# The scan of a Mamba-2 layer, written channel-major: two heads side by side, two gate projections moved into the convolution loop, fixed PSUM banks

## The reference, cut to what matters

```python
proj = h @ w_in                       # 1024 -> z 2048 | xbc 2560 | dt 32
z, xbc, dt = split(proj)
xbc = silu(causal_depthwise_conv(xbc, conv_w, conv_b))        # 4 taps
xs, bm, cm = split(xbc)               # x: 32 heads of 64; B, C: 2 groups of 128
dt = softplus(dt + dt_bias);  a = -exp(a_log)
# scan in two chunks of 128 tokens (c = 0, 1); l, s are tokens within a chunk
a_cs   = cumsum(dt * a)
decay  = exp(a_cs[l] - a_cs[s]) for s <= l, else 0
y_diag = einsum(C B^T, decay, x * dt)                         # within a chunk
states = einsum(B, exp(a_cs[last] - a_cs), x * dt)            # chunk 0's end state
y_off  = einsum(C, states, exp(a_cs))                         # into chunk 1
y = y_diag + y_off + d_skip * xs
g = y * silu(z);  g = g * rsqrt(mean(g*g per group) + eps) * norm_w
out = g @ w_out                       # 2048 -> 1024
```

## Time and profile before

| | us |
|---|---|
| median of 3 runs (lowest to highest) | 1395.65 (1393.22 to 1397.87) |
| the profiled execution, its own time | 1398.21 |
| its span | 1396.4 |
| TensorE busy | 1333.6 (95%) |
| VectorE busy | 855.3 (61%) |
| ScalarE busy | 666.5 (48%) |
| mean granted TensorE clock | 0.981 of full speed |

### The profile page before, as it was taken

The page is one execution under the profiler, slowest core; times in us unless marked ns, Lnnn a source line. Parts: engine busy times, 40 slices in busy tenths (PEclk is TensorE's granted clock), DMA queues, the critical chain, the costliest instruction groups (busy, mean ns, idle before and its releaser), DMA issues.

```text
span 1396.4 us, 20308 instructions
## 1 busy us (share of the span) xinstructions
PE 1333.6 (95%) x8604; PEld 1212.5 (87%) x8604; DVE 855.3 (61%) x1125; ACT 666.5 (48%) x834; POOL 40.5 (3%) x59
## 2 busy tenths in 40 slices
PE   5999999999999999998997999999999999999997
PEld 5888789999899889997997988899989888899996
DVE  4677665554554665555898786655555776665553
ACT  4454454443354454443765554544444545454442
POOL 2000000000000000000101110000000000000000
PEclk9899999999999999999998999999998999999999
DMA  7643365556554475552773444655525143375540
GB/s 239 169 126 141 101 216 191 187 194 192 157 155 143 166 239 187 194 169 91 240 231 108 137 160 139 231 195 192 186 87 211 54 143 130 123 246 190 181 151 31
DMA packets 147834, 231.06 MB, mean 165 GB/s; under 512 B 7651, under 2 KB 116493, under 8 KB 147744
## 3 DMA queue, kind: packets, MB, share of 16 engines
q1 hardware_dynamic: 144896, 221.66, 48.0%
q0 software_dynamic: 2848, 8.10, 2.7%
HBM read 227.08 MB, written 2.65 MB: 165 GB/s over the span
## 4 chain that ended last, share of the span: by engine, by line
PE 78%; DVE 13%; ACT 5%; issue 2%; DMA 2%; POOL 0%; SPq 0%; DVEq 0%; POOLq 0%; ACTq 0%
PE bank L501 13%; PE bank L503 13%; PE bank L502 13%; PE acc L697 11%; PE acc L698 10%; PE acc L701 10%; DVE wlo L484 5%; ACT whi L474 3%; PE bank L855 2%; DMA raw<-in_mla_w_in 1%; DMA raw<-in_mla_w_ukv 1%; PE bank L630 1%; PE bank L1305 1%; ACT junk L523 1%; DVE cacc L1503 1%
## 5 line engine op out<-in xcount | busy, mean ns | idle before, releaser
L484 DVE TENSOR_TENSOR wlo<-raw,whi 128x2048 fp32r<-128x2048 f32 (+1 forms) x209 | 466.8, 2245 | 195.6 <-ACT whi L474 195.5
L474 ACT ACTIVATE whi<-raw 128x2048 fp32r<-128x2048 f32 (+1 forms) x209 | 387.7, 1869 | 89.7 <-PE acc L701 79.3
L501 PE MATMUL bank<-hhi,whi 128*128 128x256 f32 x1448 | 414.5, 286 | 6.3 <-DVE xn L1575 3.7
L502 PE MATMUL bank<-hlo,whi 128*128 128x256 f32 x1448 | 411.3, 284 | 0.0
L503 PE MATMUL bank<-hhi,wlo 128*128 128x256 f32 x1448 | 411.2, 284 | 0.0
L501 PEld LDWEIGHTS bank<-hhi,whi 128*128 128x128 f32 x1448 | 278.3, 192 | 12.3 <-issue 8.2
L502 PEld LDWEIGHTS bank<-hlo,whi 128*128 128x128 f32 x1448 | 278.4, 192 | 3.3 <-issue 1.0
L503 PEld LDWEIGHTS bank<-hhi,wlo 128*128 128x128 f32 x1448 | 278.3, 192 | 0.2
L697 PE MATMUL acc<-whi,uhi 128*128 128x512 f32 x512 | 200.0, 391 | 1.8 <-DVE ulo L816 1.8
L698 PE MATMUL acc<-wlo,uhi 128*128 128x512 f32 x512 | 200.0, 391 | 0.0
L701 PE MATMUL acc<-whi,ulo 128*128 128x512 f32 x512 | 159.3, 390 | 0.0
(11 more groups left out here) (213 smaller groups left out, 1676.9 us busy)
## 6 DMA issues: line engine op xcount, KB each, us to landing
raw<-in_mlp_w SPq DMA_DIRECT2D x128, 1024.0 KB, 5.3
raw<-in_ssd_w_in SPq DMA_DIRECT2D x18, 1024.0 KB, 6.1
raw<-in_mla_w_o SPq DMA_DIRECT2D x16, 1024.0 KB, 5.6
raw<-in_mla_w_ukv SPq DMA_DIRECT2D x8, 1024.0 KB, 6.2
raw<-in_moba_w_qkv SPq DMA_DIRECT2D x16, 512.0 KB, 5.5
raw<-in_ssd_w_out SPq DMA_DIRECT2D x8, 1024.0 KB, 5.0
raw<-in_mla_w_uq SPq DMA_DIRECT2D x8, 768.0 KB, 8.7
raw<-in_mla_w_in SPq DMA_DIRECT2D x4, 1024.0 KB, 8.3
```

The lines of the kernel that those rows point to most:

```text
L474: nc.scalar.activation(whi[:, s, :e], raw[:, s, :e], ACT.Copy).then_inc(w_hi_done[s], 1)
L484: nc.vector.tensor_tensor(wlo[:, s, :e], raw[:, s, :e], whi[:, s, :e].bitcast(F32), ALU.subtract).then_inc(w_split[s], 1)
L501: nc.tensor.matmul(ps, lhs[0], rhs[0], start=start, stop=False)
L502: nc.tensor.matmul(ps, lhs[0], rhs[1], start=False, stop=False)
```

## The change: what it does

- Instead of [token, channel] the scan's outputs are formed as [channel, token]: the stationary operand is a head's `xdt` (128 tokens x 64 channels), the moving one its decays (128 x 128). Two heads write the lower and the upper 64 partitions of one bank ("side by side"). The transposes back ("yT"), the copies to `y_sb` and their sum fall away.
- The state is no longer formed. Chunk 0's part in chunk 1 is a product of `dxdt` with a third block `cross` = exp(running sum) times C1 B0^T (`cbx`), which is loaded by GpSimd, taken through exp by ScalarE and multiplied by `cbx` by VectorE in each round.
- The subtraction in the decays becomes a maximum over a whole 128 x 1024 block on VectorE, and the difference goes into ScalarE's exp as a bias, which needs one instruction per head: 16 of 128 x 128 a round.
- The gate projections z0 and z1 stand in the convolution loop after cv5 and cv7, as do the decays and inputs of round 0. Gates of round q are finished in round q+1; the output units 4 to 7 follow scan 3.
- Banks are fixed: y in 0 and 1, xT and z in 2 and 3; cv8 in 1, cv9 in 2.
- The sums of squares move from GpSimd to VectorE (`gate_sum`).
- Which unit is split where is written out by hand (`split_early`, `split_late`).

```diff
-        prevT = xn[:, 1, 512:1024]
-        y_sb = junk[:].rearrange("p (c n) -> p c n", c=T)
+        cross = junk[:].rearrange("p (h n) -> p h n", h=8)
...
+            def gate_unit(n, bank=None):
+                unit(("z", n), KD, 256, cols(w, 256 * n, 256 * (n + 1)))
+                jobs.add(("z", n), bank, ready=used(("z", n)))
+
+            def turned_inputs(q):
+                jobs.add(("xT", q, 0), 2)
+                jobs.add(("xT", q, 1), 3)
+
             for n in range(10):
...
-                jobs.add(("cv", n), ready=used(("cv", n)))
+                jobs.add(("cv", n), {8: 1, 9: 2}.get(n), ready=used(("cv", n)))
...
+                if n in (5, 7):
+                    gate_unit((n - 5) // 2)
+                if n == 7:
+                    turned_inputs(0)
+            for q in range(4):
                 if q:
+                    gate_unit(2 * q, 2)
+                    gate_unit(2 * q + 1, 3)
+                jobs.add(("y", 2 * q), 0)
+                jobs.add(("y", 2 * q + 1), 1)
+                if q < 3:
+                    turned_inputs(q + 1)
                 for n in out_units[q]:      # now {0: [], 1: [0, 1], 2: [2, 3], 3: [4, 5, 6, 7]}
                     unit(("so", L, n), 2, DM, rows(A["ssd_w_out"][0], 256 * n, 256 * (n + 1)))
...
+            split_early = {1: so[1], 2: ("z", 5), 3: ("z", 7)}
+            split_late = {1: ("z", 5), 2: so[3], 3: so[5]}
...
+            def scan(n):
+                q = n // 2
+                ps = open_job(te, ("y", n))
+                for i in range(2):
+                    hh = [4 * (n % 2) + 2 * i + a for a in range(2)]
+                    ch = [slice(h * SSD_HD, (h + 1) * SSD_HD) for h in hh]
+                    dst = [ps[a * SSD_HD:(a + 1) * SSD_HD, i * SEQ:(i + 1) * SEQ] for a in range(2)]
+                    for a in range(2):
+                        nc.tensor.matmul(dst[a][:, tok(0)], xdt[:, 0, ch[a]], dec[:, (2 * q) % 4, hh[a], :],
+                                         start=True, stop=True)
+                    for a in range(2):
+                        nc.tensor.matmul(dst[a][:, tok(1)], xdt[:, 1, ch[a]], dec[:, (2 * q + 1) % 4, hh[a], :],
+                                         start=True, stop=False)
+                    for a in range(2):
+                        mm = nc.tensor.matmul(dst[a][:, tok(1)], dxdt[:, ch[a]], cross[:, hh[a], :],
+                                              start=False, stop=True)
+                mm.then_inc(ready(("y", n)), 1)
...
+            for q in range(4):              # TensorE, after cv9
                 if q:
                     proj(("z", 2 * q))
                     proj(("z", 2 * q + 1))
+                job_copied(te, ("xT", q, 0))
+                job_copied(te, ("xT", q, 1))
+                te.wait_ge(dx_done, q + 1)
+                te.wait_ge(dec_ready, 2 * (q + 1))
+                te.wait_ge(cross_ready, q + 1)
+                scan(2 * q)
+                scan(2 * q + 1)
+                if q < 3:
+                    turn_inputs(q + 1)
                 for n in out_units[q]:
...
+                if q >= 2:
+                    sums(q - 2)
...
+            def decays(q):                  # ScalarE
+                for c in range(T):
+                    b = (2 * q + c) % 4
+                    act.wait_ge(dec_diff, 2 * q + c + 1)
+                    for hh in range(8):
+                        ins = nc.scalar.activation(dec[:, b, hh, :], dec[:, b, hh, :], ACT.Exp, scale=-1.0,
+                                                   bias=tokv[:, 2 + c, 8 * q + hh:8 * q + hh + 1])
+                    ins.then_inc(dec_exp, 1)
+
+            def cross_decay(q):
+                act.wait_ge(cross_loaded, 16 * (q + 1))
+                nc.scalar.activation(cross, cross, ACT.Exp, scale=-1.0).then_inc(cross_exp, 1)
...
+                if n in (5, 7):             # in ScalarE's convolution loop, behind silu(n - 1)
+                    gate_silu((n - 5) // 2)
+                if n == 5:
+                    decays(0)
+                    cross_decay(0)
...
+            decays(1)
+            for q in range(1, 5):
+                for n in (2 * q - 2, 2 * q - 1):
+                    gate_square(n)
+                    gate_hi(n)
                 if q < 4:
+                    cross_decay(q)
+                    if q < 3:
+                        decays(q + 1)
+                    act_splits(act, split_early[q], 0)
+                    gate_silu(2 * q)
+                    gate_silu(2 * q + 1)
+                    act_splits(act, split_late[q], 0)
+            act_splits(act, ("so", L, 7), AHEAD - 1)
...
+                if n in (4, 6):             # in VectorE's convolution loop, behind conv(n)
+                    diffs((n - 4) // 2)
+                if n in (5, 7):
+                    dve_splits(dve, ("z", (n - 5) // 2))
+                if n == 7:
+                    decay_cb(0, 0)
+                    decay_cb(0, 1)
+                    cross_cb(0)
+                if n == 8:
+                    scaled_inputs(0)
...
+            for q in range(1, 5):
                 if q < 4:
+                    scaled_inputs(q)
+                for n in (2 * q - 2, 2 * q - 1):
+                    gate(n)
+                if q == 1:
+                    decay_cb(1, 0)
+                    decay_cb(1, 1)
+                for n in (2 * q - 2, 2 * q - 1):
+                    gate_sum(n)
+                    gate_lo(n)
                 if q < 4:
                     if q < 3:
                         diffs(q + 1)
+                    cross_cb(q)
                     if q < 3:
                         decay_cb(q + 1, 0)
                         decay_cb(q + 1, 1)
+                    dve_splits(dve, split_early[q], 0)
+                    if q == 3:
+                        mean_square(0)
+                        half_residual()
+                    dve_splits(dve, split_late[q], 0)
+            dve_splits(dve, ("so", L, 7), 0)
+            mean_square(1)
+            dve_splits(dve, ("so", L, 7), AHEAD - 1)
```

More of the change, by code:

```diff
@@ L179, in build @@
         headc = sb("headc", [SSD_H, 4])
-        tokv = sb("tokv", [P, 6, SSD_H])
+        tokv = sb("tokv", [P, 5, SSD_H])
         g_ms = sb("g_ms", [P, SSD_G, T])
@@ L228, in build @@
             CT = sb("CT", [P, SSD_G, SEQ], F32, stage)
-            Btok = sb("Btok", [P, SSD_G, P], F32, stage)
+            cbx = sb("cbx", [P, SSD_G, P], F32, stage)
             cbm = sb("cbm", [P, SSD_G, T, P], F32, stage)
@@ L381, in plan_ssd @@
                     jobs.add("cb")
[L382 to L386, removed]
-                if q:
[L388 to L399, removed]
-                if q in (2, 4):
-                    jobs.add(("ss", q // 2 - 1))
+                    jobs.add("cbx")
+                if n in (5, 7):
[3 more added lines that the diff above has]
+            for q in range(4):
+                if q:
+                    gate_unit(2 * q, 2)
[4 more added lines that the diff above has]
+                    turned_inputs(q + 1)
                 for n in out_units[q]:
                     unit(("so", L, n), 2, DM, rows(A["ssd_w_out"][0], 256 * n, 256 * (n + 1)))
+                if q >= 2:
+                    jobs.add(("ss", q - 2), 3)
         bias_in_mla = "moba" in kinds and kinds[0] == "mla"
@@ L1260, in build @@
         DT, EXP, U, LN, DD, DEC, DTO, ACS = range(8)
+        so_of = {L: {n: ("so", L, n) for n in range(8)} for kind, L, i in stages if kind == "ssd"}
+        split_early, split_late = {}, {}
+        for so in so_of.values():
+            split_early = {1: so[1], 2: ("z", 5), 3: ("z", 7)}
+            split_late = {1: ("z", 5), 2: so[3], 3: so[5]}
         def pe_ssd(te, j, L):
@@ L1340, in pe_ssd @@
+                        mm = nc.tensor.matmul(ps[:, g * P:(g + 1) * P], BT[:, g, tok(0)], CT[:, g, tok(1)],
+                                              start=True, stop=True)
+                    mm.then_inc(ready("cbx"), 1)
+                if n in (5, 7):
+                    proj(("z", (n - 5) // 2))
+                if n == 7:
+                    turn_inputs(0)
+            for q in range(4):
+                if q:
                     proj(("z", 2 * q))
-                    te.wait_ge(dx_done, q + 1)
@@ new lines, in half_residual @@
+            def half_residual():
+                dve.wait_ge(grstd_done, 1)
+                for t in range(T):
+                    if t == 0:
+                        dve.wait_ge(acc_done, acc_rounds[j])
+                    else:
+                        dve.wait_ge(*used(("so", L, 3)))
+                    for half in range(2):
+                        c = slice(512 * half, 512 * half + 512)
+                        nc.vector.scalar_tensor_tensor(out=x[:, t, c], in0=acc[t][half][:],
+                                                       scalar=g_rstd[:, 0, t:t + 1], in1=x[:, t, c], op0=ALU.mult,
+                                                       op1=ALU.add).then_inc(ssd_half, 1)
```

288 lines of the change are left out of this document (99 added, 189 removed).

## The result

The changed kernel takes 1421.15 us (median of four runs, 1418.78 to 1421.76) beside 1396.72 us (four runs, 1393.22 to 1397.87): 1.0172 times as long, 95% interval 1.0157 to 1.0187. It is slower, as forecast, but by 24.4 us where 14.5 were forecast, and outside the range of 1399 to 1417. The profiled execution took 1421.76 us, its span is 1419.7 us and its mean clock 0.976; before they were 1398.21, 1396.4 and 0.981. So 23.3 us of span are to be found.

What follows compares the result with a forecast made beforehand. TensorE, 95% busy, was taken to bound the kernel. The terms -14.1 + 10.7 + 2.1 + 9.0 + 6.8 = +14.5 us, on the median 1395.65, gave a forecast of 1410 us, range 1399 to 1417.

Steps and rivals of the forecast that it cites:

- The three waits: TensorE idle in the SSD stage: 8.2 us before cv9, 6.5 us before z6, 4.1 us before so6.
- late at the residual: Behind so6, VectorE still has so7, up0 and up1 to split and reaches the residual 0.7 us late.
- Nothing outside this stage changes: Outside the SSD stage the kernel stays as it was; no time was entered for it.
- TensorE's own work: In the scan, a round falls from 6.1 to 5.2 us: 3.7 us less over four rounds, 0.2 added for `cbx`.
- the overlap: In the scan, the two heads of a pair overlap wholly, so a round takes 2.6 us; chance 0.28.
- The rival: Scan pairs overlap; of 4 x 2.6 us only 3.8 us come out, giving 1406 us; chance 0.28.
- The short waits: Round 1: TensorE waits 0.35 us before z2 and 1.8 us before scan 2 of the rounds, 2.1 us together.
- The small exps: ScalarE's decays: 16 exps of 128 columns at 0.25 us each, 4.1 us a round; upper end 6.4.
- the rival of 0.40 us: Small exps cost 0.40 us, each `decays` 2.4 us longer, +4.8 us in all, giving 1415 us; chance 0.12.
- The drain of 1.38 us: ScalarE's table reload: by the skill's estimate, the two chains with a reload would each be about 1.38 us longer.
- The clock: Low TensorE clock behind the waits: +2.5 us after cv9, +2.5 after z6, +2.0 after so6 (0 to 2.5).
- old losses: SSD stage of the old order: waits and low clock lose 3.1 + 3.7 + 2.9 + 0.9 = 10.6 us, all gained.

Runs made afterwards that it cites:

- split_early: Changed kernel with the weight splits of z7 and so7 moved so that they don't stand behind `gate_hi`: 1402.86 us, ratio 1.0047.
- xt_early: Changed kernel with `scaled_inputs(0)`, which frees bank 2, placed on VectorE ahead of the block products: 1412.58 us, ratio 1.0116.
- layout_before: Kernel before the change with its tiles moved 128 bytes lower, where the changed kernel has them: 1404.22 us, ratio 1.0056.
- same_half: Changed kernel with one head's three scan products, then the other's, all written to the lower 64 partitions: 1417.36 us in its one run.
- old_decays: Changed kernel with the earlier decays: small subtractions with a maximum on VectorE and two large exps a round on ScalarE: 1413.21 us, ratio 1.0120.
- pairs_apart: Changed kernel with the three scan products of one head issued first, then the three of the other: 1417.81 us, ratio 1.0153.
- layout_back: Changed kernel with `tokv` given its sixth row again, so later tiles lie where they lay before the change: 1410.92 us, ratio 1.0104.

## Why the prediction was right or wrong

**The three waits: right.** cv9 0.83 + 7.76 us (8.2 forecast), z6 6.71 (6.5), so6 4.43 (4.1), each ended by the instruction that was named. split_early and xt_early show the causes. The 0.7 us that VectorE was to be late at the residual didn't come: TensorE stands 0.17 us before the MLP's first product, 0.18 before the change.

**"Nothing outside this stage changes": wrong, and the step that failed.** It is a term that the sum has at nothing without a reason. The step looked at instructions, not at addresses. The smaller `tokv` moved `uhi`, `ulo`, `ohi` and `olo`; layout_before puts it at 7.6 us by itself (that is outside the stage and within it), of the 9.9 us by which the forecast fell short. The diff had the line (`[P, 6, SSD_H]` to `[P, 5, SSD_H]`); I read it as an edit without cost.

**TensorE's own work: wrong, with little effect on the time.** I took 5.2 us a round, since no row showed an overlap, and gave the overlap 0.28. It is 2.65 us between the first and the last product of a round. That is 10.2 us less than forecast over four rounds (the term is -13.6 with `cbx`, not -3.5), and next to none of it was kept. The rival priced what could come out of it at 3.8 us; by same_half it is 1 to 3. The Trainium skill, "TensorEngine Tiling (Array Packing)", section Key Properties, has column tiles multiply in parallel: the trace agrees, 0.054 us a record on average against 0.109 with one half. It also has the array drain when the tiling mode changes: ahead of scan 0 the start is 0.21 us behind that of the product before it (757.84 to 758.05), where the products are 0.12 apart and so is the step from a unit to the transposes of 128 columns (733.89 to 734.01), so such a drain costs at most some 0.1 us here.

**The short waits: too few and too short.** The rows of z2 and scan 1 in the kernel after:

```profile
763.16 0.36 PE L505 MATMUL bank<-hhi,whi 128*128 128x256 f32 x1 [1.25 <-DVE xn L1554]
776.50 0.44 PE L1294 MATMUL bank<-dec,xn 128*64 128x128 f32 x4 [1.59 <-DVE junk L1545]
```

With xT(2, 0) 3.28 (z2's bank, freed by ScalarE), so2 1.11 and so4 2.14 they are 9.4 us. The sum had 2.1: z2 with 0.35 and scan 1 (`cross_cb(1)`) with 1.8. The other three, 6.5 us, it had at nothing. I had laid out VectorE's and ScalarE's queues against the serial scan; with short scans each is late. In same_half, where the scans are serial, these five sum to 0.51 + 0.45 + 0.73 = 1.7 us, near the 2.1. So the prediction's ledger fits the kernel that it assumed.

**The small exps: too low.** 4.80 us, not 4.1. The rows for it were 0.25 apart for two instructions; sixteen are 0.30 apart. What a microsecond of them is worth was about right: the rival of 0.40 us made 4.8 us of 2.4 us more a round, twice as much; old_decays takes 2.8 us a round off ScalarE, adds 0.9 to VectorE, and is 8 us faster, of which 5.5 are left without the clock behind the waits it didn't touch. The drain of 1.38 us that the Trainium skill, "ScalarE: Activation LUTs", section What ACT_TABLE_LOAD costs, sets beside the load isn't in the trace: the copy ends at 717.53, the load starts at 717.55, and the exp 1.30 us after that.

**The clock: 10.8 us, not 7.0** (2.5 + 2.5 + 2.0). Behind cv9, z6 and so6 it cost 2.6, 2.4 and 2.5 us, near the forecast; xT(2, 0) added 1.7 and so4 1.6. The last is not a fixed price: pairs_apart has 1.86 us of idle before so4 and loses nothing there (output units 4 and 5 in 11.39 us, 12.96 in after), and split_early and layout_back lose nothing there behind the same 2.1 us.

Inside the stage: own work and old losses -24.2, waits +29.1, clock +10.8, some 0.8 for its 192 slower output products at 4.3 ns, together +16.5; measured +17.75. Another 1.2 us stand between the first transpose and the first unit of the convolution (18.1 us instead of 17.0), where nothing was changed and the wait before it is the same 3.67 us; two executions differ by that much there in the clock.

**The sum as a whole.** It fell 9.9 us short: 7.6 for the addresses, 10.1 the other way for the scan's own work, 0.9 for the three large waits, 7.3 for the short ones, 3.8 for the clock, -0.7 for the residual, and 1.2 as just said, together 10.0. That the scan's own work nearly cancels against the short waits and the clock is in part one effect (short scans wait longer), as same_half shows, and in part luck.

## What to carry to other kernels

On a kernel bound by TensorE, price an edit by whether every operand and every bank is ready when TensorE asks; shorter products gained next to nothing here until the other engines' queues were put in the order of TensorE's needs, and then most of it (19 us less than before, of the 24.2 that own work and old losses are worth). Weight preparation that is queued behind an instruction which waits for TensorE turns into a stall of its full length, however early its buffer was free. And when an edit changes a tile's size, print the addresses of all the others: 128 bytes cost 0.56%, nearly all of it in stages that nobody had touched.

## What was not expected of the hardware

- An output product (128x128 stationary, 128x512 moving, float32r) comes 228.0 ns behind the one before with both operands at the same offset within 512 bytes and 232.3 ns otherwise (durations 391 and 394 to 396 ns): 7.6 to 8.9 us on 2208 products, in six kernels with four placements. I have no cause for it.
- Products that write different halves of the partitions not only overlap when they are neighbours in the program: records of the one half overtake earlier ones of the other. In pairs_apart the fourth product of the program starts with the second, at 758.32, and ahead of the third, at 758.54.
